# Seven block products of eight in an input projection, in two token passes, and half of the merge logits moved out of a recurrence

## What is computed

```python
h = rmsnorm(x, g_pre[l])
proj = h @ w_in[l]
(c_q, c_kv, k_pe, gate_a, hq, hf, hi, gate_b, merge_logits) = jnp.split(proj, split_at, axis=-1)
...
q_dec = qc * jnp.exp(cum)
k_inv = kc * jnp.exp(-cum)
...
gates = jax.nn.sigmoid((merge_logits + b_gate[l]).astype(jnp.float32)).astype(x.dtype)
m = gates[..., :D_MODEL] * y_a + gates[..., D_MODEL:] * y_b
```

## Time and profile before

| what | us |
|---|---|
| median of 3 runs | 2309.71 |
| lowest, highest | 2307.43, 2317.5 |
| span of the profiled execution | 2308.5 |
| stage A ends, stage B begins (first instruction of B) | 684.83 |
| stage B ends | about 1181 |
| attention, merge and output | 1181 to 2308.5 |

### The profile page before, as it was taken

The page is one execution under the profiler, slowest core; times in us unless marked ns, Lnnn a source line. Parts: engine busy times, 40 slices in busy tenths (PEclk is TensorE's granted clock), DMA queues, the critical chain, the costliest instruction groups (busy, mean ns, idle before and its releaser), DMA issues.

```text
span 2308.5 us, 32797 instructions
## 1 busy us (share of the span) xinstructions
PE 2194.0 (95%) x11569; PEld 1815.6 (79%) x11569; DVE 1049.9 (45%) x1877; ACT 901.4 (39%) x1675; POOL 341.3 (15%) x324
## 2 busy tenths in 40 slices
PE   7999999999999999999978989999999998999998
PEld 5888887778878888888866778778888777778886
DVE  6111000100004555444446657677777766664652
ACT  7212111100114444344433326565666666443441
POOL 2222224031201111111111330000000022000000
PEclk9999999999999999999999999999999999999999
DMA  5222122131312323333266764333212336574751
GB/s 188 82 70 74 63 76 77 69 127 54 101 63 83 95 91 95 100 95 94 77 207 220 263 206 95 71 71 74 51 41 60 73 93 208 176 229 130 204 155 64
DMA packets 215332, 257.99 MB, mean 112 GB/s; under 512 B 37713, under 2 KB 136465, under 8 KB 212753
## 3 DMA queue, kind: packets, MB, share of 16 engines
q1 hardware_dynamic: 186000, 203.59, 31.0%
q10 hardware_dynamic: 23552, 42.50, 5.0%
...
...
## 4 chain that ended last, share of the span: by engine, by line
PE 52%; DMA 5%; DVE 4%; ACT 4%; issue 3%; SPq 1%; POOL 1%; ACTq 0%; DVEq 0%; POOLq 0%
PE bankD L74 5%; PE bankD L76 5%; PE bankD L75 5%; PE bankE L74 4%; PE bankE L76 3%; PE bankE L75 3%; PE turn_rest L2074 3%; PE scores L74 3%; PE scores L76 2%; PE scores L75 2%; PE o_acc L2086 2%; DMA e_g_in<-gateTok 2%; PE o_acc L2087 2%; PE turn_first L2074 2%; ACT probs L1888 2%
## 5 line engine op out<-in xcount | busy, mean ns | idle before, releaser
L74 PE MATMUL bankD<-hT_hi,shared_w_hi 128*128 128x512 f32 x512 | 211.6, 413 | 5.2 <-PEq L1166 5.2
L76 PE MATMUL bankD<-hT_hi,shared_w_lo 128*128 128x512 f32 x512 | 201.3, 393 | 0.0
L74 PE MATMUL bankA<-hT_hi,shared_w_hi 128*128 128x512 f32 x512 | 201.0, 393 | 0.0
L75 PE MATMUL bankD<-hT_lo,shared_w_hi 128*128 128x512 f32 x512 | 200.4, 391 | 0.0
L76 PE MATMUL bankA<-hT_hi,shared_w_lo 128*128 128x512 f32 x512 | 199.6, 390 | 0.0
L75 PE MATMUL bankA<-hT_lo,shared_w_hi 128*128 128x512 f32 x512 | 199.5, 390 | 0.0
L1868 DVE TENSOR_REDUCE small_chunk_min<-scores 128x1 f32<-128x512 f32 (+2 forms) x320 | 181.2, 605 | 35.2 <-PE scores L76 21.2
L1888 ACT ACTIVATE probs<-scores,small_least 128x1024 f32<-128x1024 f32 (+2 forms) x192 | 167.1, 870 | 12.7 <-DVE small_least L1875 11.6
L74 PE MATMUL bankA<-wt_hi,hT_hi 128*128 128x512 f32 x384 | 151.4, 394 | 5.5 <-DVE shared_v_raw L498 2.2
L76 PE MATMUL bankA<-wt_hi,hT_lo 128*128 128x512 f32 x384 | 150.5, 392 | 0.0
L2022 DVE TENSOR_TENSOR pT<-turn_rest,pT 128x512 fp32r<-128x512 f32 (+2 forms) x208 | 126.2, 625 | 53.3 <-ACT pT L1988 53.3
...
## 6 DMA issues: line engine op xcount, KB each, us to landing
shared_w_raw<-in_w_in_dram SPq DMA_DIRECT2D x32, 512.0 KB, 4.3
...
shared_w_lo<-hgTok SPq DMA_DIRECT2D x16, 512.0 KB, 3.4
...
```

The source lines that it names most:

```text
L74: pe.matmul(out, a_hi, b_hi, start=first, stop=False)
L75: pe.matmul(out, a_hi, b_lo, start=False, stop=False)
L76: return pe.matmul(out, a_lo, b_hi, start=False, stop=last)
```

## The change

Stage A now runs in two passes of 1024 tokens, and `x` is loaded, normalised and transposed once for each. In a pass, a unit "F" makes 256 columns of feature-major output and a unit "T" a segment of 512 columns in token-major form. Each splits tokens, depth and columns in two, and makes the result from seven products of blocks and of sums of blocks (the Winograd form of Strassen's scheme). F's product is 12 matmuls of 512 columns, T's is 48 matmuls of 256 columns. The sums of input blocks (S1 to S4) are made once per pass; the sums of weight blocks are made on GpSimd for every unit, in place in the raw weights. Half of the merge logits, those of the first 1024 tokens, are 8 F units between the passes; the recurrence keeps the other half, 16 groups of three matmuls per unit. Recurrence inputs have places of their own (`early`), with double-buffered weights and a raw copy of the values that GpSimd splits in stage B.

The order of the units, and how TensorE makes a product:

```diff
+PASSES = 2
+HALF_T = TPB
+KH = KD // 2
...
+FW, TW = P, W // 2
+
+A11, S2, A12, S3, S1, A22, S4, A21 = range(8)
+SUM_OF = (0, 1, 0, 1, 2, 1, 2)
+OPENS = (0, 1, 4)
+P1_AT, U2_AT, C11_AT, U3_AT, C22_AT, C21_AT, C12_AT = range(7)
+N_PROD = 7
+
+
+def projection_units():
+
+    first = [("F", n) for n in (T_HQ, T_HQ + 2, T_HF, T_HF + 2)] + [("T", s) for s in range(len(SEG_COLS))]
+    first += [("F", n) for n in (KQ, 0, 2, 4)] + [("R", T_PE)]
+    return [(0, *u) for u in first] + [(0, "F", T_ML + 2 * g) for g in range(KD)] + [(1, *u) for u in first]
+
...
+                def product(u, i):
+                    pe.wait_ge(w_ready, OB[u] + i + 1)
+                    operand_of_pass(u, i)
+                    accumulator_free(u, i)
+                    b = 2 * SUM_OF[i]
+                    hh, hl, wh, wl = h_of(i, plain_hi, sums_hi), h_of(i, plain_lo, sums_lo), slot_hi(u, i), slot_lo(u, i)
+                    opens = i in OPENS
+                    if kind(u) == "F":
+                        for k in range(KH):
+                            for a, c in ((wh, hh), (wh, hl), (wl, hh)):
+                                last = pe.matmul(bank[:, b], a[:, k], c[:, k], start=opens and k == 0 and a is wh and c is hh,
+                                                 stop=k == KH - 1 and a is wl, skip_group_check=True)
```

SP loads one unit's raw weights (`w_raw` of F: 1024 KB, one place; `t_raw` of T: 2048 KB) once the last of the seven operands before it in that place is split:

```diff
+                def load_raw(u):
+                    if kind(u) == "T":
+                        s = SEQ[u][2]
+                        if kind(u - 1) == "T":
+                            sp.wait_ge(w_ready, OB[u])
+                        else:
+                            h_complete(sp, SEQ[u][0])
+                        sp.dma_start(t_raw[:], w_v[:, :, SEG_COLS[s]:SEG_COLS[s] + W]).then_inc(t_raw_in, 16)
+                        return
+                    before = [v for v in range(u) if kind(v) != "T"]
+                    if before:
+                        sp.wait_ge(w_ready, OB[before[-1] + 1])
+                    if kind(u) == "R":
+                        sp.dma_start(rope_raw, w_v[:, :, C_PE:C_PE + ROPE]).then_inc(f_raw_in, 16)
+                    else:
+                        n = SEQ[u][2]
+                        sp.dma_start(w_raw, w_v[:, :, column(n):column(n) + 2 * P]).then_inc(f_raw_in, 16)
...
+                def loads_of(u):
+
+                    later = [v for v in range(u + 1, N_UNITS) if (kind(v) == "T") == (kind(u) == "T")]
+                    if later and not (kind(u) == "T" and SEQ[u][2] == len(SEG_COLS) - 1):
+                        load_raw(later[0])
+                    if SEQ[u][1:] == ("F", T_HQ + 2):
+                        load_raw(u + 3)
```

GpSimd's sums of weight blocks, ScalarE's rounding and VectorE's subtraction for operand m, and VectorE's reads of PSUM. ScalarE and VectorE work through the products in order; after product m each does its reads and then prepares operand m + 3 (`after(m)`), in four slots:

```diff
+                def first_sums(u):
+                    (b11, b12), (b21, b22) = raw_blocks(u)
+                    n, room = 4 * full_before(u), sum_room(u)
+                    raw_arrived(u)
+                    if u > 0 and kind(u - 1) != "R":
+                        pool.wait_ge(w_ready, OB[u - 1] + 5)
+                    if kind(u) == "T" and SEQ[u][0] == 1 and SEQ[u][2] == 0:
+                        pool.wait_ge(c_sq_added, 12)
+                    pool.tensor_tensor(room, b12, b11, ALU.subtract).then_inc(w_sum, 1)
+                    pool.wait_ge(w_sum, n + 1)
+                    pool.tensor_tensor(b12, b22, b12, ALU.subtract).then_inc(w_sum, 1)
+                    pool.wait_ge(w_ready, OB[u] + 1)
+                    pool.tensor_tensor(b11, b22, room, ALU.subtract).then_inc(w_sum, 1)
+
+                def last_sum(u):
+                    (b11, b12), (b21, b22) = raw_blocks(u)
+                    pool.wait_ge(w_sum, 4 * full_before(u) + 3)
+                    pool.wait_ge(w_ready, OB[u] + 3)
+                    pool.tensor_tensor(b21, b21, b11, ALU.subtract).then_inc(w_sum, 1)
...
+                    if i in (1, 3, 4, 5):
+                        act.wait_ge(w_sum, 4 * full_before(u) + {4: 1, 3: 2, 1: 3, 5: 4}[i])
+                    act.activation(slot_hi(u, i), operand(u, i), ACT.Copy).then_inc(w_hi_ready, 1)
...
+                def lo_of_operand(m):
+                    u = UNIT_OF[m]
+                    dve.wait_ge(w_hi_ready, m + 1)
...
+                    dve.tensor_tensor(slot_lo(u, i), operand(u, i), slot_hi(u, i).bitcast(F32), ALU.subtract).then_inc(w_ready, 1)
...
+                    if i in (U2_AT, U3_AT, C22_AT, C21_AT, C12_AT):
+                        dve.wait_ge(prod_done, m + 1)
+                    if i == U2_AT:
+                        squared(u, 3)
+                        dve.wait_ge(act_read, 2 * u + 1)
+                        wait_stored(dve, u, stores_awaited(u, 1))
+                        dve.tensor_tensor(u2, b2, first, ALU.add).then_inc(dve_read, 1)
+                    elif i == U3_AT:
+                        squared(u, 1)
+                        wait_stored(dve, u, stores_awaited(u, 2))
+                        dve.tensor_tensor(u3, b2, first, ALU.add).then_inc(dve_read, 1)
...
+                def after(m):
+                    u = UNIT_OF[m]
+                    i = m - OB[u]
+                    p = SEQ[u][0]
+                    combine(m)
...
+                        lo_of_operand(m + 3)
+                    if u in U_CQ and i in (4, 5):
```

In pass 2 the input sums are made while the last merge logits and the first unit run:

```diff
+                for u in range(N_UNITS):
+                    p = SEQ[u][0]
+                    if u == U_LAST_ML - 1:
+                        lo_of(1, A21)
+                        pool.wait_ge(c_sum_split, 2 * PASSES)
+                        for c in range(len(CHUNKS[1])):
+                            sum_of_second_half(1, c)
+                            difference_of_halves(1, c)
+                    if u == U_P1:
+                        for c in range(len(CHUNKS[1])):
+                            sum_less_first(1, c)
+                    if kind(u) != "R":
+                        first_sums(u)
+                    if u == 0:
+                        lo_of(0, A21)
+                        for c in range(len(CHUNKS[0])):
...
+                    if u == U_LAST_ML and i == 0:
+                        lo_of(1, A11)
+                    if u == U_LAST_ML and i == 2:
+                        lo_of(1, A12)
+                    if u == U_LAST_ML and i == 3:
+                        hi_of(1, S2)
+                        lo_of(1, S2)
+                    if u == U_LAST_ML and i == 5:
+                        hi_of(1, S3)
+                        lo_of(1, S3)
+                    if u == U_LAST_ML and i == 6:
+                        lo_of(1, S1)
+                    if u == U_P1 and i == 2:
+                        lo_of(1, S4)
```

In stage B:

```diff
+    NJ = 2
...
-    AT_TURN_K, AT_SCORES, AT_UPDATES, AT_INTRA, AT_INTER, AT_TURN = 4, 5, 10, 18, 22, (26, 28)
+    AT_TURN_K, AT_SCORES, AT_UPDATES, AT_INTRA, AT_INTER, AT_TURN = 1, 1, 3, 8, 10, (13, 15)
...
-                    sp.wait_ge(w_split, n * 2 + 2)
-                    load_weights(n + 1)
+                    sp.wait_ge(v_split, n + 1)
+                    load_v(pair + (blk + 1) // NB, (blk + 1) % NB)
+                    sp.wait_ge(w_split, n + 2)
+                    if not last_pair or blk < NB - 2:
+                        load_weights(n + 2, blk % 2)
...
-                def round_weights(n, half):
-                    if half == 0:
-                        dve.wait_ge(w_arrived, n * 16 + 16)
-                        dve.wait_ge(half_used, n + 1)
-                    else:
-                        dve.wait_ge(prod_done, n * NB + NB)
-                    ks = slice(half * KD // 2, (half + 1) * KD // 2)
-                    dve.tensor_copy(w_hi[:, ks], w_raw[:, ks]).then_inc(w_hi_done, 1)
+                def round_weights(n, u, trips):
+                    dve.wait_ge(w_arrived[u], trips * 16 + 16)
+                    dve.wait_ge(prod_done, n * NJ - NJ)
+                    dve.tensor_copy(w_hi[u], w_raw[u]).then_inc(w_hi_done, 1)
...
                         lower_bounded(pair + (blk + 1) // NB, (blk + 1) % 2, pair * (NB // 2) + (blk + 1) // 2)
+                        round_weights(n + 1, (blk + 1) % 2, pair * (NB // 2) + (blk + 1) // 2)
                     dve.wait_ge(ket_hi, n + 1)
```

1180 lines of the change are left out of this document (727 added, 453 removed).

## The result

Before 2310.3 us (2307.4 to 2317.5), after **2423.6 us** (2421.7 to 2426.1): ratio 1.048, 95% interval 1.046 to 1.050. Slower, as forecast, but the forecast was 2353 with a range up to 2390, so the time lies outside it.

The account below looks back on a forecast made before the run. The prediction took TensorE, busy 95% of the span, as the bound; stage A +184.4 us and stage B -139.7 summed to +44.7 on 2308.5, giving 2353 us, with a range of 2295 to 2390.

Parts of the forecast that it names:

- T's matmuls: Stage A: 2016 matmuls of 256 columns with starts 0.12 us apart, 241.9 us instead of 261.2: -19.3.
- The load: Stage A's weight chain: 1024 KB of raw weights land in 5.3 us, within 4.3 and 6.2.
- The loop of F: Stage A's weight chain takes 21.4 us a unit against 19.05 of products, 2.35 late 19 times: +44.7 us.
- TensorE's wait for ket: Stage B: the loop through ket takes 21.5 us a unit, 1.8 over the 19.7 of TensorE's work.
- Product 1 of unit 0: Start of stage A: product 1 can start at 56.6 us, once VectorE has rounded and split S2.
- Stage A, start: Sums, splits and load bring unit 1's product 3 to 91.2 us; overhead of 61 us instead of 33: +28.
- Stage A, rest: -12: The 24 us for 64 tiny matmuls and waits in stage A become about half: -12 us.
- pass change +23.5: Stage A, between passes: transposes on TensorE and queues on GpSimd and VectorE make products late: +23.5 us.
- T to T: Stage A: the weight loop for T takes about 41 to 42 us against 40.3, +1 four times: +4 us.
- the forecast's loop: Stage B: 7.25 us from output transpose through ket to updates, plus 14.23 back to the transpose: 21.5 a unit.
- everything contends: Rival on the weight chain: load 6.2 and sums at 1.67 give 22.9 us a unit, +28: 2381; chance 0.21.
- The rule on shared interfaces: GpSimd's weight sums: by the skill's contention rule each costs the maximum, transition 2.9 instead of 2.35, 11 us more.

Follow-up runs that it names:

- e1: The changed kernel with VectorE splitting operand 6 ahead of its read of product 3 instead of behind it: 2400.1 us, ratio 1.038.
- f1: On top of e1, the first pass's S1, S3, S2 and S4 are summed by VectorE instead of GpSimd: 2386.6 us, ratio 1.032.
- j3: The changed kernel with only stage A's tiny latent sums and their splits retimed: 2398.4 us, ratio 1.038.
- e2: The changed kernel with the next unit's ket rounded and split before outputs are scaled in stage B, the weights' rounding behind it: 2432.7 us, ratio 1.052.
- e3: The changed kernel with VectorE rounding the next merge weights behind ket's subtraction instead of ahead of it in stage B: 2435.8 us, ratio 1.054.
- f4: The changed kernel with ket first in stage B, and the outputs' scaling and weights' rounding moved behind the states' low part: 2392.0 us, ratio 1.033.

## Why the prediction was wrong

**Right.** T's matmuls: 0.12 apart as priced (two starts of the changed kernel), and 40.32 us a unit:

```profile
170.01 0.28 PE L1009 MATMUL bankA<-shared_w_hi,plain_hi 128*128 128x256 f32 x1
170.13 0.28 PE L1009 MATMUL bankA<-shared_w_lo,plain_hi 128*128 128x256 f32 x1
```

The load, 5.3 forecast (KB, median us to landing):

```profile
shared_w_raw<-in_w_in_dram SPq DMA_DIRECT2D x24, 1024.0 KB, 5.4
```

The loop of F, 21.4 forecast, measured 20.9 to 21.4 and confirmed by e1. TensorE's wait for ket, 1.8 a unit forecast, 24.9 / 15 = 1.7. Product 1 of unit 0, 56.6 forecast, 59.2.

**Failed in stage A (+45).**
- *"Stage A, start"*: from product 1 to unit 1's product 3 it had loads and splits, and every GpSimd sum at 1.29. The fourth sum took 7.76 beside VectorE's work, A22 and S4 stood behind it, and product 5 waited 10.6. Product 3 of unit 1 is read at 103.8, not 91.2: +12.6. f1 shows the gate.
- *"Stage A, rest: -12"*: this term left 12 us for the tiny matmuls and every other wait, and took the tiny latent matmuls for small because they are. The latent and rope units took 115.0 in the first pass and 105.2 in the second, where their matmuls alone are 83.5 each: 53 over, where the loop and this term had 26: +27. The units with the x loads are +8. This is the largest part, and j3 got 25 back by order alone.
- *"pass change +23.5"*: six units took 155.4 where 21.4 each are 128.4: 27.0, +3.5.
- T to T had been given 4 and needed none (-4); the remaining units of F were 1 under the forecast, and from the last product to B's first instruction it was 9.3, not 10.9 (-1.5). The parts sum to +45.
- Part of each is the clock: behind the waits of stage A from 55 us on, 11 stretches, 37 us in all, have starts 0.43 apart, which is 1.2 GHz. At 2.4 they would be some 17 shorter. No term of the forecast had that.

**Failed in stage B (+20).** The wait for ket was sized right, the unit was not: 22.9 for 21.5. In TensorE's time that is 19.9 of work (forecast 19.7), 1.7 for ket, 0.3 at the states' low part (4.0 in all) and 0.8 of clock (the eight stretches at 1.2 GHz, 26 us in all, cost some 12): 22.7. No term had the last two. What sets the pace had been drawn wrong: the forecast's loop ran from the updates through 14.23 us of TensorE to the transposes, and then through ket, with the rounding as a removable link. e2 and e3 showed it to be VectorE's work from the outputs' sums to the states' low part, 15.8 to 16.9 us, and then 5.7 to 5.9 of TensorE and ScalarE to the next sums, which TensorE starts 1.0 to 2.6 late where its clock had fallen; f4 shortened it. By an estimate from the turns above, about half of the 20 us is this loop at full clock and half the clock.

**The rival "everything contends"** had the right sign and the wrong place: loads did not contend, GpSimd and VectorE did, not at 1.67 for 1.29 but at 7.76, 10.16 and, for casts, 2.83 for 0.64.

**The rule on shared interfaces.** The forecast priced the Trainium skill's rule (GPSIMD Engine Reference, 8. Key points: contention with VectorE instructions that have two SBUF inputs or run in a 2-port mode) at 11 us. Rows of this case agree with the rule and not with the price, which had been taken from the slowest of the earlier trace rows, in a stage where VectorE is busy for 236 of 487 us.
